# Conditioning loads issued ahead of the weight loads and folded later; GpSimd makes the third weight difference before a low half

## The reference, cut to what matters

```python
mod = jax.nn.silu(c) @ ada_w[l] + ada_b[l]                      # 9 x 1024 values per sequence
sh1, sc1, g1, sh2, sc2, g2, sh3, sc3, g3 = jnp.split(mod, N_MOD, axis=-1)
h = modulate(rmsnorm(x, ffn1_norm[l]), sh1, sc1)
x = x + 0.5 * g1[:, None, :] * swiglu(h, ffn1_wg[l], ffn1_wu[l], ffn1_wd[l])   # D_FF = 2816
...                                                              # attention with sh2, sc2, g2
x = x + 0.5 * g3[:, None, :] * swiglu(h, ffn2_wg[l], ffn2_wu[l], ffn2_wd[l])
x = rmsnorm(x, final_norm[l])
```

## Time and profile before

| | |
|---|---|
| time, median of 3 runs | 3060.56 us (3052.28 to 3063.91) |
| profiled execution, its own time | 3053.62 us |
| its span, first to last instruction | 3051.8 us |
| mean granted TensorE clock | 0.983 |
| busy: TensorE matmul, GpSimd, VectorE, ScalarE | 95%, 73%, 57%, 51% of the span |

### The profile page before, as it was taken

How to read it: one execution, slowest core, us unless ns; L and a number is a source line. 1 busy time by engine, 2 the same in 40 slices (tenths; PEclk the granted TensorE clock), 3 DMA queues, 4 the chain that set the end, 5 groups by cost and what they waited for, 6 DMA issues and landing times.

```text
span 3051.8 us, 49300 instructions
## 1 busy us (share of the span) xinstructions
PE 2889.3 (95%) x16057; PEld 2655.0 (87%) x16057; DVE 1745.2 (57%) x3002; ACT 1554.7 (51%) x2585; POOL 2227.9 (73%) x1116
## 2 busy tenths in 40 slices
PE   6899999989999999997989999999999998999998
PEld 3899999989999988885656667989999998999998
DVE  5666766666667756886544332275444457544545
ACT  6533444543434466765767776444444345444444
POOL 1788888788888864333547666678898987889883
PEclk9999999999999999998999999999999999999999
DMA  7233232324233353556323234432212232221223
GB/s 277 102 92 117 83 116 88 116 97 124 84 99 101 92 178 119 152 152 161 114 56 85 61 89 145 128 100 94 84 55 82 74 116 93 64 83 55 82 79 148
DMA packets 378610, 323.46 MB, mean 106 GB/s; under 512 B 22780, under 2 KB 325743, under 8 KB 378479
## 3 DMA queue, kind: packets, MB, share of 16 engines
q1 hardware_dynamic: 375342, 320.21, 34.5%
q10 hardware_dynamic: 3136, 1.57, 0.2%
HBM read 263.29 MB, written 58.43 MB: 105 GB/s over the span
## 4 chain that ended last, share of the span: by engine, by line
POOL 40%; issue 23%; PE 19%; DMA 8%; DVE 4%; ACT 2%; SPq 1%; POOLq 0%; ACTq 0%; DVEq 0%
POOL W_lo L2391 20%; POOL quart L2413 9%; POOL XT_r L1844 8%; DMA quart<-in_ffn_wu 5%; PE PS L519 3%; PE PS L520 3%; PE PS L521 3%; DMA quart<-in_ffn_wd 2%; POOL qsum L2413 2%; PE PS L2848 1%; PE PS L2850 1%; PE PS L2849 1%; SPq L2274 1%; ACT W_hi L2385 1%; PE PS L2909 1%
## 5 line engine op out<-in xcount | busy, mean ns | idle before, releaser
L2391 POOL TENSOR_TENSOR W_lo<-quart,W_hi 128x1024 fp32r<-128x1024 f32 x384 | 938.5, 2460 | 246.0 <-ACT W_hi L2385 246.0
L2848 PE MATMUL PS<-SL,W_hi 128*128 128x384 f32 x2112 | 716.3, 339 | 48.3 <-POOL W_lo L2391 36.8
L2850 PE MATMUL PS<-SL,W_lo 128*128 128x384 f32 x2112 | 710.2, 336 | 0.0
L2385 ACT ACTIVATE W_hi<-quart 128x1024 fp32r<-128x1024 f32 x384 | 403.0, 1059 | 603.1 <-POOL quart L2413 225.6
L2849 PE MATMUL PS<-SL,W_hi 128*128 128x384 f32 x2112 | 710.2, 336 | 0.0
L2054 DVE SCALAR_TENSOR_TENSOR XT<-PS,mod,XT 128x384 f32<-128x384 f32 (+1 forms) x840 | 418.2, 526 | 271.9 <-PE PS L2910 167.5
L2848 PEld LDWEIGHTS PS<-SL,W_hi 128*128 128x128 f32 x2112 | 399.6, 189 | 63.0 <-POOL W_lo L2391 44.9
L1844 POOL TENSOR_TENSOR XT_r<-XT,XT_r 128x512 fp32r<-128x512 f32 x224 | 286.8, 1285 | 178.3 <-ACT XT_r L1696 177.7
L2849 PEld LDWEIGHTS PS<-SL,W_hi 128*128 128x128 f32 x2112 | 399.5, 189 | 1.0 <-issue 1.0
L2850 PEld LDWEIGHTS PS<-SL,W_lo 128*128 128x128 f32 x2112 | 399.6, 189 | 0.0
L2413 POOL TENSOR_TENSOR quart<-quart 128x1024 f32<-128x1024 f32 x128 | 316.9, 2476 | 10.4 <-DVE qsum L2413 1.2
(11 more groups left out here) (314 smaller groups left out, 6445.8 us busy)
## 6 DMA issues: line engine op xcount, KB each, us to landing
quart<-in_ffn_wg SPq DMA_DIRECT2D x176, 256.0 KB, 3.1
quart<-in_ffn_wu SPq DMA_DIRECT2D x176, 256.0 KB, 3.4
quart<-in_ffn_wd SPq DMA_DIRECT2D x160, 256.0 KB, 2.9
ada_r<-in_ada_w SPq DMA_DIRECT2D x128, 192.0 KB, 3.0
raw<-in_w_out SPq DMA_DIRECT2D x30, 512.0 KB, 3.9
ada_w_sb<-in_ada_w SPq DMA_DIRECT2D x6, 2048.0 KB, 19.1
XT<-scr_xt SPq DMA_DIRECT2D x8, 1536.0 KB, 8.3
scr_xt<-XT SPq DMA_DIRECT2D x4, 2688.0 KB
```

Of the source, the lines that this page charges most:

```text
L2385: act.activation(W_hi[:, slot_of(S, u), :], unit_src(u), ACT.Copy).then_inc(unit_hi, 1)
L2391: pool.tensor_tensor(W_lo[:, slot_of(S, u), :], unit_src(u), W_hi[:, slot_of(S, u), :].bitcast(F32), ALU.subtract) \
L2848: pe.matmul(out, w_hi, m_hi, start=j in PRODUCT_OPENS and kp == 0, stop=False, skip_group_check=True)
L2850: mm = pe.matmul(out, w_lo, m_hi, start=False, stop=kp == 3, skip_group_check=True)
```

## The change

Four edits, all in the feed-forward lists:

1. **SP.** All eight conditioning loads are issued ahead of the next spot's quarters (they were six, then A11Q, then two). A11Q's load waits for low half 3 (`S.unit(4)`) and not for sum 3, and A12Q's load stands ahead of `unpark`.
2. **VectorE.** Four of the conditioning sums stand ahead of the first combine in `GA` and `GB` alike (in `GB` it was three), and `ada_mods` moves from right behind `ada_fold` to behind the last low half of the made operands.
3. **TensorE.** `ada_reduce` moves from behind product T3 to behind product T4, and writes in bank BY = 2 instead of bank 7; the next spot's product in that bank (B21, or the third tile of B11 in `DN`) waits until `ada_mods` is done.
4. **GpSimd.** Sum 3 stands right behind sum 2 and ahead of lo 3 (it needs only that unit 1 is made). After `SO` of h = 0 and 2, sums 1 and 2 of the next pass's first spot are made at once, ahead of that spot's lo 1.

```diff
@@ ada_reduce, ada_mods
-                mm = pe.matmul(PS[j * QB:(j + 1) * QB, ADA_BANK, ADA_COL:ADA_COL + 2 * ADA_PER], fold[:, :],
+                mm = pe.matmul(PS[j * QB:(j + 1) * QB, BY, ADA_COL:ADA_COL + 2 * ADA_PER], fold[:, :],
...
@@ ffn_loads, spot
-                for k in range(6) if S.ada() else ():
+                for k in range(KD) if S.ada() else ():
                     ada_load(sp, S, k)
-                spot_load(sp, N, A11Q, sum_ready, S.sums(4))
-                for k in range(6, KD) if S.ada() else ():
-                    ada_load(sp, S, k)
+                spot_load(sp, N, A11Q, unit_ready, S.unit(4))
                 spot_load(sp, N, A21Q, unit_ready, S.unit(5))
                 spot_load(sp, N, A22Q, unit_ready, S.unit(6))
+                spot_load(sp, N, A12Q, unit_ready, S.unit(7))
                 if last:
                     unpark(sp, S.h, 0)
-                spot_load(sp, N, A12Q, unit_ready, S.unit(7))
@@ ffn_loads, single
-                sp.wait_ge(sum_ready, S.sums(4))
+                sp.wait_ge(unit_ready, S.unit(4))
@@ spot_sum
             if no == 3:
-                eng.wait_ge(unit_ready, S.unit(4))
+                eng.wait_ge(unit_ready, S.unit(2))
@@ ffn_pool, spot
+                ahead = S.first and S.h != 2
                 if not (S.first and S.h == 0):
                     spot_lo(pool, S, 1)
+                if not ahead:
                     spot_sum(pool, S, 1)
                 spot_lo(pool, S, 2)
-                if not (S.first and S.h == 0):
+                if not ahead:
                     spot_sum(pool, S, 2)
+                spot_sum(pool, S, 3)
                 spot_lo(pool, S, 3)
-                spot_sum(pool, S, 3)
...
+                if S.kind == SO and S.ahead() is not None:
+                    spot_sum(pool, S.ahead(), 1)
+                    spot_sum(pool, S.ahead(), 2)
@@ ffn_dve, gate_up
-                for k in range(before) if S.ada() else ():
+                for k in range(KD // 2) if S.ada() else ():
                     ada_sum(dve, S, k)
...
-                    for k in range(before, KD):
+                    for k in range(KD // 2, KD):
                         ada_sum(dve, S, k)
                     ada_fold(dve, S)
-                    ada_mods(dve, S)
...
                 made_lo_dve(dve, S, T2)
+                if S.ada():
+                    ada_mods(dve, S)
@@ spot_product (and the same at B11, i == 2, of down_product)
                 elif j == B21:
                     pe.wait_ge(st_hid, B.ready(MADE_ORDER.index(T3) + 1))
+                    if B.ada():
+                        pe.wait_ge(ada_mod_kept, B.ada_turn() + 2)
@@ ffn_pe, gate_up
-                    if S.ada() and j == T3:
+                    if S.ada() and j == T4:
                         ada_reduce(pe, S)
```

More of the change, by code:

```diff
@@ L538, in ada_mods @@
             dve.wait_ge(ada_red, S.ada_turn() + 1)
-            out = PS[:, ADA_BANK, ADA_COL:ADA_COL + 2 * ADA_PER].rearrange("p (j s) -> p j s", s=2)
+            out = PS[:, BY, ADA_COL:ADA_COL + 2 * ADA_PER].rearrange("p (j s) -> p j s", s=2)
             for c in range(NCH):
@@ L2739, in gate_up @@
             def gate_up(S):
-                turned, before = S.first and S.h % 2, 4 if S.kind == GA else 3
+                turned = S.first and S.h % 2
                 if S.kind == GB:
@@ L2895, in down_product @@
                     pe.wait_ge(st_hid, G.ready(MADE_ORDER.index(T3) + 1))
+                    if G.ada():
+                        pe.wait_ge(ada_mod_kept, G.ada_turn() + 2)
                 if n == B21 and i == 1:
```

## The result

The changed kernel takes **2988.22 us** (median of four runs, 2987.88 to 2990.22) against 3058.58 for the kernel before (median of four runs, 3052.28 to 3063.91): a ratio of 0.9772, 95% interval 0.9752 to 0.9792. The profiled execution took 2988.48 us, its span is 2986.7 us and its mean granted clock 0.987.

The account below looks back on a forecast made before the run. TensorE was taken as busy nearly throughout, losing 51.1 us mostly to conditioning-spot stops for VectorE. Gains 46.3 + 2.5 + 4.5 = 53.3 off 3053.62 gave 3000.3, moved to 3004 us for the four-execution average; range 2990 to 3020.

Parts of the forecast that it names:

- the baseline: Whole kernel: the profiled execution's forecast, 3000.3, was lifted toward the 3057.6 average of four executions, giving 3004 us.
- term 3: GpSimd's order: sum 3 fills the pause before lo 3, gaining 2.5 of 3.3 us (0 to 3.3).
- term 1: 16 conditioning spots: the stop at line 532 goes, its 51.1 us less 4.8 for the reduce, gaining 46.3 (43 to 51).
- term 4: First groups and SO: GpSimd's order pays or costs directly, together +4.5 us, ends -9 and +12.
- Term 2: SP's load queue: A11Q's load behind load 7 leaves at 289.6 instead of 289.21, A22Q's is released 1.3 earlier; no cost.
- T2 waits for lo 3, which comes 1.15 later: Three GB and SO spots: about half is won back at T3, 0.5 us lost each, -1.5.
- it alone covers all 16 stops as they are: Conditioning spots: the reduce behind T4 gives VectorE 4.16 us more against a longest stop of 3.4.
- Every slack above is at least 1.5 us: Argument against half of the removed stop coming back, for instance at B21 or in VectorE's combine.
- The boundaries lose by the turn-taking: Rival at the pass boundaries: GpSimd's moved sums slow VectorE, 10.6 us less there, 2 in the first spot; 3017, chance 0.17.
- the full 4.3: Per boundary: two VectorE instructions turn long beside sums 1 and 2, 4.3 us landing on VectorE by the exclusive-lock rule.
- Half of the stop returns elsewhere: Rival: waits return at B21 or VectorE's combine, or the clock stays low; 23 us less, 3027, chance 0.08.
- Slower by load 7 holding the quarters: Rival on SP: load 7 some 8 us late delays the next spot's quarters; 3075 us, chance 0.04.

## Why the prediction was right in its sign and too small in its size

The forecast of 3004 is 15.8 us above 2988.2. Two steps make this up: the sum said 53.3 where the traces differ by 65.1 (11.8), and the baseline added 4.0. Of the 11.8, `SO` and the end make 9.6 and the first groups 5.2, term 3 gives 0.8; term 1 takes 1.3 off and the start and the middle 2.5. Terms 2 and 4 together gave 16.8 where term 4's upper end was 12, and the low end of the range was the sum of the upper ends.

**Term 2, SP, "No cost": the step that failed.** The prediction worked this term out for A11Q and A22Q only, and said nothing of the fourth load, A12Q, which the change takes out from behind `unpark`. That edit was costed at nothing. Undone, it costs 9.9 us by the medians and 8.1 by the lengths of the three stretches; made alone, it gains 12.3 there. That is about the size of the miss of the sum. The way to it was open: ScalarE's hi 1 in `SO` of h = 2 stood 7.56 us for this load in the trace before. I had looked at the two `SO` only for what lo 4 and lo 3 do, and gave them +1 each where they gained 2.9 and 5.2, and the end nothing where it gained 3.6. The order of lo 3 and sum 3 has no part in it: with lo 3 first everywhere `SO` keeps its 47.4.

**Term 4, the first groups: mis-sized in both directions.** Without `SO` and the end, the first groups were given +2.5 (2 for the first spot, 1 for each start of h = 1 and 3, less the 1.5 for T2). Measured are +2.9 and -0.7 in h = 0, +6.2 and +0.7 in h = 1, +2.9 and +1.4 in h = 3, and -5.2 and -0.6 in h = 2: +7.7 in all, from the unrounded lengths.
- The start of h = 1 and 3 was mis-sized. The kernel without the early sums loses 6.7 and 5.4 there. I had capped the gain at 2.3 by the last operand of T2 and did not look for waits elsewhere in the spot. In the first `GA` of h = 1 TensorE had stood for low halves four times up to the next spot's first product, 8.5 us in all. After the change none of these is left; the stops for which the trace names no engine grew there from 1.6 to 4.8.
- The first `GA` of h = 2 was not worked out. Sum 3 ahead costs 5.2 there, shown by the kernel that puts lo 3 first in it alone. "T2 waits for lo 3, which comes 1.15 later" was the right rule, applied to three other spots with GpSimd's short duration. There it measured 0.7 to 0.9 each, and 0.3 to 0.6 with the `DN` behind them, against my 0.5. Beside VectorE the instruction is 3.8 long.
- The first `GA` of h = 0 gave +2.9 for +2. Seven of the eight kernels with sum 3 first there took 39.4 to 39.9 us and the six with lo 3 first 40.8 to 42.8, so the order does gain there. How much is not exact: the eighth took 42.51 with nothing but A12Q's load moved back, which leaves this spot's lists as they are, and four of the six had a clock of 0.71 over product T3, which alone takes some 1.5 us.
- The start of the kernel (-1.1) and the middle (-1.4) are not explained by an edit; they also vary between the other kernels (77.1 to 80.1, and 942.4 to 948.6).

**Term 1, the conditioning spots: 45.0 for 46.3, by a working that was half right.** The size is that of the stop, and the reduce costs 0.38 us and not 0.3 (16 x 0.08 = 1.3, the whole difference). But "it alone covers all 16 stops as they are" fell: the later place alone gained 30.3. It covers the wait at line 532 and leaves VectorE as late as it was, so the down product's B21 waits for VectorE's tail. "Every slack above is at least 1.5 us" was worked out at the times of a kernel whose TensorE lost some 3 us in each spot; TensorE at full pace takes that slack away. The edits are interchangeable, and no part owns the 45 us: the loads alone gain 41.3 on the kernel before, GpSimd's new order with SP's other edits gains 35.0 with neither conditioning edit, and on top of that order either conditioning edit gives the last 10.

**Term 3, GpSimd's order: 3.3 for 2.5, but counted in the second feed-forward alone.** It filled the pause as described. What the prediction missed is that the same 1.1 us stand in the conditioning spots ahead of A11Q's load, and so ahead of loads 6 and 7. That this path carries the 35 us is read from the rows; the runs show the gain of GpSimd's order and A11Q's wait together, and that A12Q's load alone gives 3.9 there, less than the 9.5 between its own two stretches.

**The baseline.** I moved the profiled execution's forecast up by 4.0, to the average of four executions before, and expected the same spread after. The spread went instead: the four runs after lie within 2.3 us, and the profiled execution (2988.48) is at their median. That a change which removes what scatters takes the slow end of the old spread with it fits this; no run isolates it.

**The rivals.** *The boundaries lose by the turn-taking* did not come true: VectorE's 128x1536 instruction in GpSimd's former pause went from 1.74 to 2.38 us and the next one to 1.84, together 0.7 more and not 4.3, and the spot gained 6.2. GpSimd and VectorE at the start of h = 1:

```profile
571.52 3.92 POOL L2411 TENSOR_TENSOR quart<-quart 128x1024 f32<-128x1024 f32 x1
575.52 3.79 POOL L2411 TENSOR_TENSOR quart<-qsum,quart 128x1024 f32<-128x1024 f32 x1
```

```profile
574.68 2.38 DVE L2209 TENSOR_TENSOR SLf<-SLf 128x1536 f32<-128x1536 f32 x1
579.09 1.84 DVE L2209 TENSOR_TENSOR X4f<-SLf 128x1536 f32<-128x1536 f32 x1
```

GpSimd bears the longer durations (3.92, 3.79), VectorE little. So "the full 4.3" did not come out here, and "they take turns", read from 3.9 for both, doesn't say which engine pays. *Half of the stop returns elsewhere* is in part what the later place alone shows: a third of the gain was missing, and the largest wait was at B21, as the rival said. The clock did not stay low (1.00 in both stretches), and GpSimd's order or the loads take the waits away. *Slower by load 7 holding the quarters* did not happen: A11Q's load leaves 13.8 us into the `GA` (280.86 - 267.09), 0.7 later than before, and the looped groups have no wait. SP in that spot:

```profile
280.86 0.38 SPq L2274 DMA_DIRECT2D quart<-in_ffn_wg  x1
```

## What to carry to other kernels

When an edit moves a load past another transfer on the same queue, cost it by how long it took to land behind that transfer, even where the issuing engine never waits, and look up who waited for that load in the trace before. When a stop is removed, work out the slacks at the new pace: what was in time behind a stop may be late without it, and two edits that reach the same stop don't add. A reordering that is right in the steady spots should be costed again in the first spots of a pass, where the same instruction takes 3.8 us and not 2.4.

## What the runs showed of the hardware

- The clock after a stop. Behind the stops at line 532, of up to 3.4 or 3.5 us, product T4 took 5.6 to 5.9 us with a mean granted clock of 0.71 to 0.74 in 7 of 16 spots of the kernel before and in 4 of 16 of the kernel with A12Q's load first. In the other spots of both it took 4.3 at a clock of 1.00; full pace is 4.16. The length of the stop alone doesn't tell which: one of 1.65 us was followed by the low clock and one of 2.9 was not. Behind stops of up to 1.1 us (neither conditioning edit) no T4 of 16 had it. That such stops cost differently each time fits the scatter, which no run isolates: 26.8 us over eight runs of the kernel with A12Q's load first and 8.3 to 20.4 over the sets of seven to eleven runs of the kernel before, against 1.5 to 8.3 us over four or five runs each of the twelve kernels whose stops there are short or gone.
- Two loads of 256 KB issued within 3.6 us behind a 1.5 MB transfer on the same queue took 5.7 to 8.6 us to land, against medians of 3.1 and 3.4 us.
- The four small matmuls of `ada_reduce` between two products at full pace cost 0.38 us each time.
- VectorE's operand instructions and GpSimd's share the loss unevenly: beside them GpSimd's 128x1024 took 3.8 to 3.9 us instead of 2.40, VectorE's 128x1536 1.84 and 2.38 in one place and 3.90 in another instead of 1.74.
